# A third buffer for the high parts of the u tiles while the picks are made

## The reference

```python
q = (xt @ wq).reshape(T, PEER_HEADS, 2, PEER_HALF)           # 8 heads, 2 x 128
s = jnp.einsum('thpd,hpnd->thpn', q, keys)                   # 128 keys a half
ts, ti = lax.top_k(s, 16)
cand_s = ts[:, :, 0, :, None] + ts[:, :, 1, None, :]
best_s, pos = lax.top_k(cand_s (256 a head), 16)
idx = cand_i[pos]; gate = softmax(best_s)
hu = einsum(u[idx], x); act = gelu(hu) * gate                # 16384 experts of 1024
out = einsum(act, v[idx])
```

## Time and profile before

| | us |
|---|---|
| median of three runs | 1717.11 |
| lowest, highest | 1716.94, 1720.28 |
| the profiled execution, its own time | 1719.37 |
| its span, first to last instruction | 1717.6 |
| TensorE busy | 1635.3 (95%) |
| VectorE busy | 1442.4 (84%) |
| ScalarE busy | 782.0 (46%) |

### The profile page before, as it was taken

One profiled execution on the slowest core, in us unless ns is written; L12 is line 12 of the kernel. 1 busy time (PEld: TensorE's weight loads), 2 busy tenths in 40 slices (PEclk: granted clock), 3 DMA queues, 4 the chain that ended last, 5 costly groups with the idle time before them and its releaser, 6 DMA issues.

```text
span 1717.6 us, 22970 instructions
## 1 busy us (share of the span) xinstructions
PE 1635.3 (95%) x8269; PEld 1396.6 (81%) x8269; DVE 1442.4 (84%) x2707; ACT 782.0 (46%) x1310; POOL 567.0 (33%) x414
## 2 busy tenths in 40 slices
PE   8999899999999999999999999988999999999998
PEld 6876555667999999999999899987777778787787
DVE  4487887866877899989988899948989989999897
ACT  4222223321244444447988899962333333333332
POOL 0000000000003344444545454524545445545450
PEclk9999999999999999999999999998999999999999
DMA  6114222134436899997999999999999999999994
GB/s 218 50 49 40 26 74 86 62 119 139 148 117 231 320 316 341 339 325 267 373 360 356 373 393 384 389 374 395 398 403 398 398 404 400 404 403 401 403 389 170
DMA packets 155351, 482.37 MB, mean 281 GB/s; under 512 B 26031, under 2 KB 43119, under 8 KB 153063
## 3 DMA queue, kind: packets, MB, share of 16 engines
q1 hardware_dynamic: 99943, 279.57, 45.7%
q0 software_dynamic: 55296, 201.35, 31.1%
HBM read 426.17 MB, written 54.42 MB: 280 GB/s over the span
## 4 chain that ended last, share of the span: by engine, by line
PE 56%; DVE 17%; DMA 17%; ACT 7%; issue 3%; SPq 1%; DVEq 0%; POOL 0%; ACTq 0%; POOLq 0%
PE ps L824 17%; PE ps L968 16%; DMA raw<-in_v 9%; PE ps L567 6%; DMA gelu_matrix<-gest 5%; PE ps L778 5%; PE ps L583 4%; DVE lo L1556 3%; PE ps L944 3%; ACT hi L1090 3%; DVE acc L1725 2%; ACT Gs L1266 1%; DVE ring L1721 1%; DVE caccb L1424 1%; ACT gA L1248 1%
## 5 line engine op out<-in xcount | busy, mean ns | idle before, releaser
L1090 ACT ACTIVATE hi<-raw 128x1024 fp32r<-128x1024 f32 x256 | 270.6, 1057 | 350.7 <-PE ps L968 175.5
L1328 POOL DMA_INDIRECT ring<-in_u,idx x192 | 276.8, 1441 | 438.7 <-DVE hu L1721 277.0
L1556 DVE TENSOR_TENSOR lo<-raw,hi 128x1024 fp32r<-128x1024 f32 x256 | 313.5, 1225 | 114.0 <-ACT hi L1090 112.3
L1328 POOL DMA_INDIRECT ring<-in_v,idx x192 | 277.6, 1446 | 282.2 <-DVE acc L1725 269.0
L824 PE MATMUL ps<-xh,hi 128*128 128x384 f32 x1024 | 351.9, 344 | 12.1 <-DVE lo L1556 11.6
L824 PE MATMUL ps<-xl,hi 128*128 128x384 f32 x1024 | 344.1, 336 | 0.0
L824 PE MATMUL ps<-xh,lo 128*128 128x384 f32 x1024 | 344.1, 336 | 0.0
L968 PE MATMUL ps<-hi,ah 128*128 128x512 f32 x768 | 241.4, 396 | 25.9 <-DVE lo L1556 12.3
L1725 DVE SCALAR_TENSOR_TENSOR acc<-ring,hu,acc 128x1024 f32<-128x1024 f32 x192 | 245.8, 1280 | 0.1
L968 PE MATMUL ps<-lo,ah 128*128 128x512 f32 x768 | 237.9, 391 | 0.0
L968 PE MATMUL ps<-hi,al 128*128 128x512 f32 x768 | 237.3, 390 | 0.0
(11 more groups left out here) (223 smaller groups left out, 1953.2 us busy)
## 6 DMA issues: line engine op xcount, KB each, us to landing
raw<-in_uT SPq DMA_DIRECT2D x128, 512.0 KB, 7.0
raw<-in_v SPq DMA_DIRECT2D x128, 512.0 KB, 9.1
wring<-in_wblk SPq DMA_DIRECT2D x58, 512.0 KB, 3.5
gelu_matrix<-gest SPq DMA_DIRECT2D x64, 384.0 KB, 8.5
gate_matrix<-Gs SPq DMA_DIRECT2D x16, 1536.0 KB, 8.0
gel<-gelu_matrix SPq DMA_DIRECT2D x64, 384.0 KB, 8.6
Gl<-gate_matrix SPq DMA_DIRECT2D x64, 384.0 KB, 11.1
wring<-in_wblk SPq DMA_DIRECT2D x16, 256.0 KB, 2.6
```

What stands on the lines that cost most here:

```text
L1090: nc.scalar.activation(hi[:, s % 2, :], raw[:, s % RAWS, :], ACT.Copy).then_inc(s_hi, 1)
L1328: pool.indirect_dma_start(ring[:, r % SLOTS, :], None, table, bass.IndirectOffsetOnAxis(idx[:, t, c:c + 1], 0)).then_inc(g_in[r % SLOTS], 16)
L1556: nc.vector.tensor_tensor(lo[:, s % 2, :], raw[:, s % RAWS, :], hi[:, s % 2, :].bitcast(F32), ALU.subtract).then_inc(s_lo, 1)
```

## The change

A third buffer for high parts, `hi_third`, is laid into the region of the gates stage's buffers, where in the pick stages nothing is held. u tiles 0 to 61 use the three buffers in turn (s % 3), all later ones the two of before. ScalarE makes high(n+3) behind the gelu of tile n up to step 58; step 59 makes none, step 60 makes high(62), step 61 high(63) and so on as before; high(2) is made ahead of step 0. Since high(s) no longer says that lo's buffer is free, low(s) waits for the end of tile s-2 itself, for s from 2 to 61.

```diff
+        with ExitStack() as picking:
+            picking.enter_context(nc.sbuf_tensor("until_gates", [P, 9 * D], F32))
+            hi_third = picking.enter_context(nc.sbuf_tensor("hi_third", [P, D], F32R))[:]
...
+        def high_of(s):
+
+            if s < U_GATE and s % 3 == 2:
+                return hi_third
+            return hi[:, (s % 3 if s < U_GATE else s % 2), :]
...
-                    for k, (a, b) in enumerate(((hi, xh), (hi, xl), (lo, xh))):
-                        mm = nc.tensor.matmul(out, a[:, n % 2, w], b[:, c, :], start=(c == 0 and k == 0),
+                    for k, (a, b) in enumerate(((high_of(n), xh), (high_of(n), xl), (lo[:, n % 2, :], xh))):
+                        mm = nc.tensor.matmul(out, a[:, w], b[:, c, :], start=(c == 0 and k == 0),
...
-                nc.scalar.activation(hi[:, s % 2, :], raw[:, s % RAWS, :], ACT.Copy).then_inc(s_hi, 1)
+                nc.scalar.activation(high_of(s), raw[:, s % RAWS, :], ACT.Copy).then_inc(s_hi, 1)
...
-                high(n + 2)
+                if n + 3 < U_GATE:
+                    high(n + 3)
+                elif n + 2 >= U_GATE:
+                    high(n + 2)
...
             score_out_a(NM - 1)
+            high(2)
...
                 dve.wait_ge(s_hi, s + 1)
-                nc.vector.tensor_tensor(lo[:, s % 2, :], raw[:, s % RAWS, :], hi[:, s % 2, :].bitcast(F32),
+                if 2 <= s < U_GATE:
+                    dve.wait_ge(s_hud, s - 1)
+                nc.vector.tensor_tensor(lo[:, s % 2, :], raw[:, s % RAWS, :], high_of(s).bitcast(F32),
```

## The result

The changed kernel took 1704.84 us (median of 4 runs, 1700.06 to 1708.07), beside 1718.01 for the kernel before (4 runs, the three of its table among them). The ratio is 0.9921, with a 95% interval of 0.9902 to 0.994. Applied to the 1717.11 of before it gives 1703.5 us.

The account below looks back on a forecast made before the run. TensorE was taken to bound the pick stages, with VectorE close behind. Gains of 4.44, 1.88 and 3.3 us sum to 9.6, taken from the 1717.11 us median to give 1707.5 us, with an eight-in-ten range of 1704.5 to 1712.5.

Parts of the forecast that it names:

- What bounds, and what goes: Pick stages: TensorE bounds, VectorE close behind; lows waiting for high parts may start up to 1.48 us earlier.
- Tiles 24 to 29, 39 to 44, 54 to 59: Pick-stage runs: tiles 29, 44, 59 each start 1.48 us earlier, about 0.7 idle stays; 4.44 us in all.
- Tiles 33 and 48: Pick stages: the 0.94 us lost before each of these tiles through a late low goes; 1.88 us in all.
- Tiles 7 to 18: First stretch: tile 18 starts 3.70 us earlier, less 0.4 for late raw(17); 3.3 us, ends 3.7 and 2.3.
- What it adds: Costs in the pick stages: no extra ScalarE instruction, a fulfilled VectorE wait taken at 0, upper end 0.7 us.
- Raw tiles: Pick stages: raw tiles become the next wait, leaving 6.0 us gained, 1711.1 us; chance 0.12.
- The limit of 1.3 us: Pick stages: ScalarE waits up to 1.3 us for raw tiles, hidden before the next gelu.
- above 3 would make me wrong: Sign in the profile after: ScalarE's waits for raw tiles above 3 us would show the forecast wrong.
- should a key expansion come on top: hidden: Pick stages: with the 3.6 us key expansion on top, the gelu is about 2 us late, without delaying TensorE.
- Behind the pick stages: Gates stage and v loop: start 9.6 us earlier, shifted whole, nothing given back.
- about 1.5 us of run-to-run spread (1716.94 to 1720.28 before): Whole-kernel time: the run-to-run spread allowed around the forecast, giving 1705.5 to 1710.5 us.
- the 9.6 itself: Up to the end of the pick stages: total gain of 9.6 us, summed from 4.44, 1.88 and 3.3.

Follow-up runs that it names:

- buffer_only: The changed kernel with its third buffer and added wait, but high parts made in the old order, high(n+2) behind tile n's gelu: 1719.07 us, ratio 1.001.
- rows_moved: The changed kernel with two of VectorE's 21 rows per later pick stage moved from its unbroken run to behind lows 4 and 6: ratio 0.9941.
- again_after: The changed kernel run a second time, with no edit: 1708.26 us (6 runs), ratio 0.9927.
- again2_after: The changed kernel run a third time, beside its variants: 1709.6 us (12 runs), ratio 0.9965.
- after_shift: The changed kernel with the third high buffer 2 KB further up in the same region: ratio 0.9957.
- wait_only: The kernel before with only the added wait of low parts for the end of tile s-2: ratio 0.9998.
- third_near: The changed kernel with the three high buffers side by side in one tensor and the pick's scratch in the low region: ratio 0.996.
- again_before: The kernel before run once more, with no edit: 1718.65 us (12 runs), ratio 0.9993.
- the three comparisons: The changed kernel against the kernel before, measured three times without further edits: ratios 0.9921, 0.9927 and 0.9965.

## Why the prediction was right, and where it missed

*What bounds, and what goes.* Right. buffer_only (1.001) against the changed kernel (0.9965 to 0.9921) shows that the order of the high parts carries the gain, and the waits for them went from 24 to 1.

*Tiles 24 to 29, 39 to 44, 54 to 59, forecast 1.48 each.* Measured 1.06, 1.41, 1.41. The leftover idle of about 0.7 is there (0.64 and 0.64; 0.99 before tile 29), and rows_moved shows that its cause is VectorE's own work, as said. 0.07 is missing in each, because low(25), low(40) and low(55) wait for the end of a tile that reads the third buffer. The other 0.35 of the first run stand in front of low(25): it starts 0.42 us after the gelu of tile 23, where low(40) starts 0.07 after that of tile 38, and from low(25) to tile 29 it is again 617.76 - 596.34 = 21.42 us.

```profile
595.92 0.49 ACT L1166 ACTIVATE gest<-ps 128x384 f32<-128x384 f32 x1 [1.81 <-PE ps L834]
```

```profile
596.34 1.23 DVE L1572 TENSOR_TENSOR lo<-raw,hi 128x1024 fp32r<-128x1024 f32 x1 [1.68 <-PE ps L834]
```

The same 0.35 is in again_after, again2_after and after_shift, and gone in rows_moved. What holds low(25) so long stays open.

*Tiles 33 and 48, 0.94 each.* Measured 0.82 and 0.81, with no idle left. What is missing are two slower tiles of 0.08.

*Tiles 7 to 18, 3.3.* Measured 3.1. The steps hold: VectorE still awaits the first row's landing (2.64 us), the idle before tile 11 nearly goes (0.25) and comes back before tile 12 (1.49), and raw(17) is late as the forecast had it. low(17) waited 0.98 for its high part, where the forecast took 0.4, and tile 18 starts 9.34 us after it, the chain of before:

```profile
561.13 1.22 DVE L1572 TENSOR_TENSOR lo<-raw,hi_third 128x1024 fp32r<-128x1024 f32 x1 [0.98 <-ACT hi_third L1100]
```

*What it adds.* "No instruction on ScalarE" and the wait at nothing: right (wait_only). Left out: the price of reading the third buffer from another place, 0.08 us a tile in 20 tiles. The part asked what each instruction costs and took a matmul to cost the same wherever its weights lie. Of the 1.3 us by which the pick stretch fell short, about 0.8 is this price (the rest of the 1.6 falls where VectorE is the bound), 0.35 is the late low(25) and 0.2 the first stretch.

*Raw tiles.* The limit of 1.3 us was too low: ScalarE waited 21 times, up to 2.5 us. The rule "above 3 would make me wrong" held. In the changed kernel's own profile one of these waits reached TensorE, that of high(17), worth 0.98 us of tile 18's start. The step "should a key expansion come on top: hidden" is true in the changed kernel's profile even behind two late raw tiles in a row, and false in third_near, where the first of them was 0.7 us later still.

*Behind the pick stages.* Right: nothing given back. From tile 61 to the end it is 950.2 to 955.2 us over all profiles, 952.6 to 954.0 in the three of the changed kernel and 954.5 to 955.2 in before, again_before and wait_only.

*The number.* The gain measured first lies above the forecast and the time 1.0 us below the range, while the mechanism's own gain lies below the forecast; so two sizes were wrong, in opposite directions. The step that failed is the last, the term of the range: "about 1.5 us of run-to-run spread (1716.94 to 1720.28 before)". Three runs were taken for the spread. Over 97 executions before has a standard deviation of 3.6 us; from that, the difference of two medians of four has one of about 2.8 us (an estimate), and a range for eight in ten needs about 4 us on either side for the spread alone. The other is the 9.6 itself: the trace has 8.3 up to tile 61, and at equal clock it is 8.2 +- 1.2. What is missing is the price of the third buffer's place (0.8), which the forecast took at nothing without a reason, the late low(25) (0.35) and a later high(17) (0.2). With 8.2 the time would be 1708.9, inside the range; it was luck, executions with a high clock, that put the first comparison some 5 us beyond that. By the three comparisons the gain is 13.6, 12.5 and 6.0.

## What to carry to other kernels

Where an engine that makes an operand in two steps holds up a nearly saturated TensorE, give the first step a buffer and make it a tile ahead; price the gain up to the point where the second engine's own unbroken work becomes the bound, and look there for the next few us (here two rows moved, 3.1 us). A buffer put wherever there is room is not free: look at the matmuls' step with it and without. And before a difference of half a per cent is explained, take the spread from a dozen runs, compare at equal granted clock as well as plainly, and locate the difference by stretch: a part that comes from stretches that the change does not touch is not the change's.

## What the hardware showed that was not expected

Matmuls that read their weights from a tensor over 40 KB below the other weights (by the sizes in the kernel) took 343 and 338 ns where the others took 334, and a tile 4.24 us where others took 4.16. Moving it 2 KB up or 16 KB down changed nothing, putting it beside the others removed it. Whether it is the distance, the region or the tensor of its own was not separated.

The granted clock fell behind the idle in front of tile 18 in half of the profiles of the same order, with a pause of about 2 us, and did not fall behind 2.93 us in the kernel before. The Trainium skill ("TensorE: Matmul & The Clock Gate", Part 1) has the clock follow how busy TensorE has been recently. The traces agree in this: from tile 0 on, the start of the v loop and the end of the program left out, the fourteen profiles have 39 stretches of low clock, and each comes with a pause of TensorE of 1.85 to 2.9 us. They also show that the same place in the same program may or may not bring one: in front of tile 18 the changed kernel had 1.84 us and no fall, 1.88 and 2.14 us and a fall.
